# Rounding three tiles of the output weights on GpSimd in place of ScalarE, in a hybrid attention layer

## The reference

```python
y = jnp.concatenate([rms_normalize(oa), rms_normalize(ob), rms_normalize(oc)], axis=-1)
y = y * g_branch[l].astype(jnp.float32) * jax.nn.silu(z.astype(jnp.float32))
y = jnp.einsum('bse,ed->bsd', y.astype(x.dtype), w_out[l])
x = layer_norm(DEEPNORM_ALPHA * x + y, ln_gain[l], ln_bias[l]).astype(x.dtype)
```

## Time and profile before

| | us |
|---|---|
| median of 3 runs | 500.43 |
| lowest and highest | 500.07, 501.27 |
| the profiled execution, its own time | 500.67 |
| span of the profiled execution | 498.5 |
| busy: TensorE, VectorE, ScalarE, GpSimd | 488.8, 311.0, 226.6, 70.8 |

### The profile page before, as it was taken

One profiled execution on the slowest core, in us unless ns is written; L12 is line 12 of the kernel. 1 busy time (PEld: TensorE's weight loads), 2 busy tenths in 40 slices (PEclk: granted clock), 3 DMA queues, 4 the chain that ended last, 5 costly groups with the idle time before them and its releaser, 6 DMA issues.

```text
span 498.5 us, 9771 instructions
## 1 busy us (share of the span) xinstructions
PE 488.8 (98%) x3526; PEld 448.3 (90%) x3526; DVE 311.0 (62%) x893; ACT 226.6 (45%) x511; POOL 70.8 (14%) x52
## 2 busy tenths in 40 slices
PE   8999999999999999999999999999999999999994
PEld 7999999999999988888888888899888898888883
DVE  4878644557565853434534468876767868877734
ACT  5632222112211134564545659947374656454540
POOL 0000000000000000111101100023232323231414
PEclk9999999999999999999999999999999999999998
DMA  7984453547632344532331258723333424232022
GB/s 283 376 255 127 159 180 104 193 134 248 212 126 87 105 125 131 158 99 75 95 97 50 98 164 266 233 58 104 114 101 106 135 68 151 67 116 83 1 85 84
DMA packets 51838, 67.97 MB, mean 136 GB/s; under 512 B 9552, under 2 KB 41296, under 8 KB 51792
## 3 DMA queue, kind: packets, MB, share of 16 engines
q1 hardware_dynamic: 51216, 66.31, 41.6%
q10 hardware_dynamic: 576, 1.05, 0.6%
HBM read 51.31 MB, written 16.02 MB: 135 GB/s over the span
## 4 chain that ended last, share of the span: by engine, by line
PE 90%; DVE 3%; ACT 3%; DMA 1%; issue 1%; SPq 0%; DVEq 0%; ACTq 0%
PE long_ps L1032 16%; PE o_ps L979 10%; PE wide L846 8%; PE wide L845 8%; PE wide L844 8%; PE narrow L961 5%; PE long_ps L921 5%; PE long_ps L923 5%; PE long_ps L922 5%; PE wide L949 4%; PE wide L950 3%; PE wide L855 2%; PE wide L857 2%; PE wide L856 2%; DMA x_raw<-in_x_t 1%; PE narrow L1008 1%
## 5 line engine op out<-in xcount | busy, mean ns | idle before, releaser
L846 PE MATMUL wide<-x_hi,w_lo 128*128 128x256 f32 x320 | 89.6, 280 | 0.0
L844 PE MATMUL wide<-x_hi,w_hi 128*128 128x256 f32 x320 | 89.3, 279 | 0.0
L845 PE MATMUL wide<-x_lo,w_hi 128*128 128x256 f32 x320 | 89.3, 279 | 0.0
L845 PEld LDWEIGHTS wide<-x_lo,w_hi 128*128 128x128 f32 x320 | 60.2, 188 | 0.0
L846 PEld LDWEIGHTS wide<-x_hi,w_lo 128*128 128x128 f32 x320 | 60.1, 188 | 0.0
L1113 ACT ACTIVATE spill<-turn 128x512 fp32r<-128x512 f32 x21 | 13.3, 632 | 102.7 <-DVE turn L1349 76.6
L844 PEld LDWEIGHTS wide<-x_hi,w_hi 128*128 128x128 f32 x320 | 59.8, 187 | 0.0
L1622 POOL TENSOR_TENSOR g_lo<-g_raw,g_hi 128x1024 fp32r<-128x1024 f32 x6 | 14.3, 2387 | 268.5 <-ACT g_hi L1118 268.5
L1032 PE MATMUL long_ps<-wo_hi,y_hi 128*128 128x512 f32 (+1 forms) x128 | 52.2, 408 | 0.0
L1032 PE MATMUL long_ps<-wo_lo,y_hi 128*128 128x512 f32 (+1 forms) x128 | 51.4, 402 | 0.0
L1032 PE MATMUL long_ps<-wo_hi,y_lo 128*128 128x512 f32 (+1 forms) x128 | 50.8, 397 | 0.0
(11 more groups left out here) (189 smaller groups left out, 1234.4 us busy)
## 6 DMA issues: line engine op xcount, KB each, us to landing
q_spill<-spill SPq DMA_DIRECT2D x32, 256.0 KB, 2.5
q_pair<-q_spill SPq DMA_DIRECT2D x128, 64.0 KB, 2.0
w_raw<-in_w_qkv SPq DMA_DIRECT2D x12, 512.0 KB, 5.0
x_raw<-in_x_t SPq DMA_DIRECT2D x16, 256.0 KB, 8.0
g_raw<-in_w_gate SPq DMA_DIRECT2D x8, 512.0 KB, 4.1
q_pair<-q_spill SPq DMA_DIRECT2D x32, 128.0 KB, 2.8
q_pair<-q_spill SPq DMA_DIRECT2D x128, 32.0 KB, 1.8
wo_raw<-in_w_out SPq DMA_DIRECT2D x8, 512.0 KB, 4.7
```

The lines of the kernel that those rows point to most:

```text
L844: pe.matmul(dst, w_hi[s][:, k, f], t_hi[:, k, cols], start=(k == 0), stop=False)
L845: pe.matmul(dst, w_hi[s][:, k, f], t_lo[:, k, cols], start=False, stop=False)
L846: mm = pe.matmul(dst, w_lo[s][:, k, f], t_hi[:, k, cols], start=False, stop=(k == KT - 1))
```

## The change

GpSimd computes `wo_hi` for tiles 4, 5 and 6, with a `tensor_scalar` from SBUF to SBUF, where ScalarE had an activation with a scale. VectorE still computes all eight `wo_lo`, and waits for the new semaphore for these three. In GpSimd's queue, tile 4 stands ahead of `y_lo` of branch 1 (step 33), tile 5 behind it (step 34), and tile 6 right behind tile 5 (step 35).

```diff
+WO_POOL = (4, 5, 6)
...
             for v in range(ITERATIONS):
                 for k in wo_tiles(v):
+                    if k in WO_POOL:
+                        continue
                     act.wait_ge(wo_in[k], 16)
                     act.activation(wo_hi[:, k, :], wo_raw[:, k, :], ACT.Copy, scale=g_col[:, k:k + 1])\
                        .then_inc(wo_rounded, 1)
...
                 for k in wo_tiles(v):
-                    dve.wait_ge(wo_rounded, k + 1)
+                    if k in WO_POOL:
+                        dve.wait_ge(wo_rounded_pool, WO_POOL.index(k) + 1)
+                    else:
+                        dve.wait_ge(wo_rounded, k + 1 - sum(m < k for m in WO_POOL))
...
+            pool.wait_ge(gate_cols_in, 32)
             for v in range(ITERATIONS):
+                for k in wo_tiles(v):
+                    if k in WO_POOL:
+                        pool.wait_ge(wo_in[k], 16)
+                        pool.tensor_scalar(wo_hi[:, k, :], wo_raw[:, k, :], g_col[:, k:k + 1], None, ALU.mult)\
+                            .then_inc(wo_rounded_pool, 1)
                 for i, j in stage_at(v, YSPLIT_AT):
```

More of the change, by code:

```diff
@@ L394, in layer @@
         o_scaled, y_rounded, y_split = sem("o_scaled"), sem("y_rounded"), sem("y_split")
-        wo_rounded, wo_split = sem("wo_rounded"), sem("wo_split")
+        wo_rounded, wo_rounded_pool, wo_split = sem("wo_rounded"), sem("wo_rounded_pool"), sem("wo_split")
         res_sum, ln_part, ln_stats = sem("res_sum"), sem("ln_part"), sem("ln_stats")
```

## The result

The changed kernel takes **503.91 us** (median of 4 runs, 502.60 to 504.33) against 500.38 us before (4 runs, 500.07 to 501.27): ratio 1.0066, 95% interval 1.005 to 1.0082. It is slower by about 3.3 us. On another occasion six runs of it had a median of 504.05 us against 500.86 (ratio 1.007, 1.0045 to 1.0096; one disturbed run of each kernel, at 536.84 and at 599.74 us, is left out). The forecast was 500.5 us, range 499.1 to 502.3. The profiled execution took 504.33 us, span 502.1.

A forecast was written before the change was run, and what follows sets the result against it. TensorE was taken as the bound, losing 1.16 us to ScalarE. Terms -0.62 - 0.20 - 0.11 + about 1.0 gave +0.1 us on the profiled 500.67, hence 500.8, or 500.5 us against the median; range 499.1 to 502.3.

The forecast's parts named there:

- What bounds the kernel: Steps 34 to 36: TensorE, busy 98% of the span, waits for ScalarE after the roundings of tiles 4, 5 and 6.
- the ceiling: Three TensorE gaps in steps 34 to 36: the change can win at most 1.16 us, 0.23% of the time.
- the first gap of 0.62 us: Step 34: TensorE's transposes start 0.62 us late, behind ScalarE's rounding of tile 4.
- What GpSimd's instruction costs: GpSimd's tensor_scalar of 1024 columns: about 1.27 us, between a write-only 1.11 and a two-input 2.39 us.
- the upper end of 2.39 us: GpSimd's rounding instruction: the measured cost of a two-input form, taken as its highest possible price.
- the dear case: Exclusion with a GpSimd instruction above 1.7 us: 501.9 to 504 us, chance 0.12.
- The exclusion: VectorE's two-operand wo_lo and GpSimd's rounding lock each other out; the later waits, holding tile 3's wo_lo 0.52 us.
- The step by step: Steps 33 to 36: VectorE's wo_lo of tile 5 ends 1.34 us later, delaying unit 34's exponentials; TensorE waits in step 36.
- The sum of +0.1 us: Steps 34 to 36: -0.62 - 0.20 - 0.11 + about 1.0 us, almost no net change.
- The slower rival: GpSimd's instruction costs the two-input 2.39 us, with exclusion, and bounds steps 33 to 36: 503.9 us; chance 0.12.
- Other work after 330 moves with TensorE: After 330 us: other work of ScalarE, VectorE and GpSimd follows TensorE; the rest was costed at nothing.
- SP's queue is untouched: Transfers on SP's queue: none is removed or moved by the change.

The follow-up runs named there:

- probe: Kernel before the change, plus 24 unused GpSimd instructions, three of each form, ahead of its loop; its one run took 502.67 us, a time not used.
- e6: Changed kernel with its three GpSimd roundings as plain casts (tensor_copy), leaving out the branch gain: 500.04 us against 501.09, ratio 0.997.
- e3: Changed kernel with only tiles 4 and 5 on GpSimd, tile 6 back on ScalarE: 501.95 us, ratio 1.003 to the kernel before.
- e4: Changed kernel with all three GpSimd roundings queued together ahead of y_lo of branch 1, in step 33: 500.54 us against 500.86 before, ratio 0.9996.
- e2: Changed kernel with only tile 4 on GpSimd, tiles 5 and 6 back on ScalarE: 500.81 us against 500.86 before, ratio 0.9998.
- e8: Second measurement of the changed kernel with all three roundings ahead of y_lo of branch 1: 499.99 us against 501.09 before, ratio 0.999.
- e9: All three roundings ahead of y_lo, and loads of gain, bias and two residual blocks moved to steps 35 to 38: 500.19 us against 500.96 before, ratio 0.999.
- e7: Changed kernel with its three GpSimd roundings as tensor_tensor against the broadcast gain column, same result: 504.20 us against 501.09 before, ratio 1.0065.
- the early order: Changed kernel with all three GpSimd roundings ahead of y_lo of branch 1, in step 33, measured twice: 500.54 and 499.99 us, ratios 0.9996 and 0.999.

## Why the prediction was wrong

**What bounds the kernel: right, and the ceiling right for one execution.** ScalarE set TensorE back in steps 34 to 36, by 1.16 us in the execution that I read. But the chain there runs through ScalarE without a break from 301.64 to 310.94, and not only through the rounding of tile 4 at 308.80, and just before it ScalarE had waited for tiles 1 and 2 to land. My text took the first gap of 0.62 us for a fixed cost, and it varies with where these landings leave ScalarE: in the two other profiles with the old roundings it is 0.05 and 0.34 us.

**The step that failed is "What GpSimd's instruction costs".** It priced the instruction at 1.27 us (its terms, 1.10 + 0.18, make 1.28), little over half of a two-input one, "if the time goes with the streams read". The instruction takes 2.85 us, above the upper end of 2.39 us that I called a bound. The probe shows that neither the operand column nor the rounding makes it so (2.78 us by a constant, 2.85 to f32), and that a cast, which also reads one stream, does take 1.05. So reading is not what the time of `tensor_scalar` goes with, and an instruction with more inputs was no upper bound for one with fewer. The range's upper end, 502.3 us, rested on that, as did 0.12 for the dear case. e6 is the check from the other side: with 1.05 us per instruction the same order gives -0.5 us of its own. Why the arithmetic form is dear stays open.

The estimates of 1.06 and 1.72 us that I drew from the Trainium skill's GPSIMD Engine Reference (§ 3.1) do not agree with this: 2.85 us. The first fits the cast (1.05 us), not the arithmetic form.

**The exclusion: right in kind, wrong in length for this instruction.** I had VectorE held to the end of GpSimd's instruction. Measured, `wo_lo` is held until a fixed time after the `tensor_scalar` began. It began 0.70 us later and took 0.20 longer (tile 3, changed kernel), 0.80 and 0.10 (e3), 0.75 and 0.16 (e4), 0.06 and 0.85 (tile 5, changed kernel): each sum is 0.90 or 0.91 us, of 2.85, and e2, e8 and e9 add five more of 0.91. Beside a cast it is 0.84 and 0.85 of 1.04 us, beside `tensor_tensor` 1.7 of 1.89. So tile 4 cost VectorE 0.2 us and not the 1.64 that I had worked out for a dear instruction, and it was the wait for the data, not the meeting, that made most of the delay. The rule of the Trainium skill's SBUF — State Buffer page (§ Who interferes with whom), that the later of the two blocks to the other's end, agrees for `tensor_tensor` and the cast, save their last 0.2 us; for `tensor_scalar` the measured 0.9 us decides. That the hold is the time in which GpSimd reads is my guess from these three lengths; no run here separates reading from writing.

**The step by step: the order was right, the place was not.** Tile 5 behind `y_lo`, `wo_lo` of tile 5 waiting for it and meeting tile 6, and work queued behind it on VectorE: all of this is in the chain. `wo_lo` of tile 5 ended 2.30 us later than before (318.34 less 0.95, against 315.09), where I had 1.34. But the first that is late is not the exponentials of unit 34 but `qo` of unit 31, which the value products of step 35 need (L974 waits for it). TensorE stops there, a step earlier than I said. That was in my own numbers too: with 1.34 us `qo` would start at 316.55, and TensorE, 0.93 us ahead, would want it at 315.87. The sum of +0.1 us hardly depends on which of the two places stops TensorE, so here a missed wait cost nothing, by luck.

**The clock: missing.** None of my cases had TensorE's clock fall. In the profile it fell after the stop of 2 us and took 1.6 us. The slower rival's 503.9 us is the measured time, but by errors that cancel: it held VectorE 1.4 us too long at tile 3, priced the instruction 0.46 us too low and left the clock out. How regular the fall is, only the runs' mean clocks hint at. A fall of 3.4 us to half lowers the mean by 0.003 to 0.004, and the kernel before lies between 0.995 and 0.999. Of the ten runs of the changed kernel two have 0.996 and are the fastest (502.60 and 502.55 us), the others 0.989 to 0.995 (503.29 to 504.90). All twelve of e3, with a stop of 1 us, lie at 0.996 or more. In e7, with a stop of 2 us, two of six have 0.996 and they are the fastest again; one of them is the profiled one, in whose trace the clock stays up through the stop. So it seems that a stop of 2 us brought the fall in most executions, not in all, and one of 1 us in none; shown in a trace are one fall (changed kernel) and one stop of 2 us without it (e7). What decides between the executions stays open.

**Behind the stretch: a cost put at nothing.** "Other work after 330 moves with TensorE" held. But the query loads did not: with the early order, one profile of two shows TensorE waiting 1.14 us for them. My text said that SP's queue is untouched, and missed that its transfers, held up by four loads of 512 KB (7 to 8 us to land, 2.5 us without those loads ahead of them), are what an earlier TensorE can run into. In the changed kernel itself, which was later and not earlier, this cost nothing.

## What to carry to other kernels

An instruction that the trace does not show has no safe upper price in a form with more inputs: time the exact form in an idle stretch of the same kernel before trusting an order that needs it in time. In an in-order queue the moved work's place can decide as much as its price: the same 2.85 us three times over cost 3.3 us behind the low part of y and nothing ahead of it, where GpSimd would have stood idle, and in the bad place a cast of 1.05 us cost nothing either. A stop of TensorE can cost its clock too (1.6 us here after 2 us), and when a stop is taken away, ask which transfer TensorE meets next. A gap that one profile shows can hang on a transfer that landed late in that execution: before two profiles are subtracted, check that the engines stood alike where the changed stretch begins.

## What the runs showed of the hardware

- GpSimd, 128x1024 from f32, where VectorE is not in the way: cast 1.05 us; `tensor_tensor` 2.39 us for two tensors, 1.90 for a tensor with itself (probe) and 1.89 against a broadcast column (e7); `tensor_scalar` 2.85 us by a column, 2.78 by a constant, and 1.57 us at 512 columns, 0.93 us at 256.
- A GpSimd instruction that began while VectorE's two-operand `w_lo` ran was itself lengthened, as at 298.23 in the kernel before: in the probe `tensor_tensor` from 1.90 to 2.22 us, `tensor_scalar` of 512 columns from 1.57 to 2.14 us.
- A two-operand instruction of VectorE is held from the start of a GpSimd instruction of 1024 columns for 0.90 us by `tensor_scalar`, 0.84 us by a cast and 1.7 us by `tensor_tensor`. Instructions of VectorE with only one operand in SBUF kept their times beside them (`prob_t<-narrow,sides`, which reads one operand from PSUM, took 0.69 us at 313.23 in the changed kernel, beside tile 5, and 0.69 us before).
- After a stop of 1.9 us the granted clock was 0.50 for 3.4 us in the changed kernel; after one of 1.97 us in e7 and one of 0.94 us in e3 it stayed at 1.00.
- The same transfer of 512 KB (tile 2 of `wo_raw`), issued at the same place, landed after 5.9 us in the kernel before, 5.3 in the changed kernel and 4.8 in e2. ScalarE stood between 0.22 and 0.57 us further ahead of TensorE when step 33 began, in the ten other profiles that are read here.
